# 512-column joint products for high and low activations in a three-part float32r matrix product kernel

## What is computed

```python
proj = n @ w_in
h = x + jnp.concatenate([gla_out, nsa_out], axis=-1) @ w_out
m = rms_norm(h, ffn_norm_g)
return h + (jax.nn.silu(m @ w_gate) * (m @ w_up)) @ w_down
```

## Time and profile before

| | |
|---|---|
| median of 3 runs | 2099.07 us (2090.81 to 2099.28) |
| the profiled execution | 2097.16 us, span 2095.2 us |
| granted TensorE clock, mean | 0.984 of full speed |
| PE busy | 2040.4 us, 97% |
| PE weight loads | 1988.4 us, 95% |
| DVE busy | 1561.3 us, 75% |
| ACT busy | 895.0 us, 43% |
| memory traffic | 434.46 MB, mean 207 GB/s |

### The profile page before, as it was taken

How to read it: one execution, slowest core, us unless ns; L and a number is a source line. 1 busy time by engine, 2 the same in 40 slices (tenths; PEclk the granted TensorE clock), 3 DMA queues, 4 the chain that set the end, 5 groups by cost and what they waited for, 6 DMA issues and landing times.

```text
span 2095.2 us, 41764 instructions
## 1 busy us (share of the span) xinstructions
PE 2040.4 (97%) x16266; PEld 1988.4 (95%) x16266; DVE 1561.3 (75%) x2056; ACT 895.0 (43%) x1178; POOL 171.9 (8%) x264
## 2 busy tenths in 40 slices
PE   7999999999999999999999998999999997999997
PEld 6999998899999999999999998998889996999996
DVE  6985576657777867787878888678887777677755
ACT  6553446554343334333333454235454444344442
POOL 0000000021000000000011111010000120000010
PEclk9999999999999999999999999999999998999998
DMA  6444453255666776666878864565556772558552
GB/s 229 161 162 136 167 184 119 101 178 205 230 228 224 261 277 222 228 224 236 272 259 295 299 224 172 172 247 197 199 171 224 262 274 105 192 204 277 195 187 98
DMA packets 119578, 434.46 MB, mean 207 GB/s; under 512 B 13216, under 2 KB 13600, under 8 KB 119216
## 3 DMA queue, kind: packets, MB, share of 16 engines
q1 hardware_dynamic: 90672, 328.11, 45.8%
q0 software_dynamic: 28800, 104.87, 14.2%
HBM read 430.83 MB, written 2.10 MB: 207 GB/s over the span
## 4 chain that ended last, share of the span: by engine, by line
PE 90%; DVE 7%; ACT 1%; issue 1%; DMA 1%; POOL 0%; SPq 0%; POOLq 0%; DVEq 0%; ACTq 0%
PE ps L565 27%; PE ps L567 26%; PE ps L566 26%; DVE w_lo L1407 2%; PE ps L644 1%; PE ps L968 1%; PE ps L639 1%; PE ps L978 1%; PE ps L683 1%; ACT w_hi L1062 0%; DVE pr L1563 0%; PE ps L674 0%; PE ps L919 0%; PE ps L650 0%; DVE rstd L1472 0%
## 5 line engine op out<-in xcount | busy, mean ns | idle before, releaser
L1062 ACT ACTIVATE w_hi<-raw 128x1024 fp32r<-128x1024 f32 x610 | 632.3, 1055 | 638.0 <-PE ps L567 625.5
L565 PE MATMUL ps<-a_hi,w_hi 128*128 128x256 f32 x3024 | 865.2, 286 | 6.3 <-DVE a_lo L1490 4.3
L566 PE MATMUL ps<-a_lo,w_hi 128*128 128x256 f32 x3024 | 858.3, 284 | 0.0
L567 PE MATMUL ps<-a_hi,w_lo 128*128 128x256 f32 x3024 | 858.1, 284 | 0.0
L1407 DVE TENSOR_TENSOR w_lo<-raw,w_hi 128x1024 fp32r<-128x1024 f32 x610 | 734.8, 1246 | 109.7 <-ACT w_hi L1062 108.6
L565 PEld LDWEIGHTS ps<-a_hi,w_hi 128*128 128x128 f32 x3024 | 583.2, 193 | 12.3 <-issue 7.5
L566 PEld LDWEIGHTS ps<-a_lo,w_hi 128*128 128x128 f32 x3024 | 583.4, 193 | 1.0 <-issue 1.0
L567 PEld LDWEIGHTS ps<-a_hi,w_lo 128*128 128x128 f32 x3024 | 583.0, 193 | 0.0
L565 PE MATMUL ps<-b_hi,w_hi 128*128 128x256 f32 x1920 | 553.6, 288 | 5.2 <-DVE b_lo L1490 4.6
L566 PE MATMUL ps<-b_lo,w_hi 128*128 128x256 f32 x1920 | 546.5, 285 | 0.0
L567 PE MATMUL ps<-b_hi,w_lo 128*128 128x256 f32 x1920 | 546.5, 285 | 0.0
(11 more groups left out here) (308 smaller groups left out, 1291.2 us busy)
## 6 DMA issues: line engine op xcount, KB each, us to landing
raw<-w_main SPq DMA_DIRECT2D x610, 512.0 KB, 4.3
side<-w_side POOLq DMA_DIRECT2D x200, 512.0 KB, 4.5
x_tok<-x_in SPq DMA_DIRECT2D x4, 512.0 KB, 7.4
ctx_tok<-ctx_tok SPq DMA_DIRECT2D x1, 2048.0 KB, 11.4
y_out<-o_tok SPq DMA_DIRECT2D x4, 512.0 KB, 3.2
table<-counts_tab SPq DMA_DIRECT2D x1, 512.0 KB, 12.9
cons<-cons_in SPq DMA_DIRECT2D x1, 478.0 KB, 10.4
table<-masks_in SPq DMA_DIRECT2D x1, 448.0 KB, 10.3
```

Source lines behind the costliest of these rows:

```text
L565: pe.matmul(out_ap, wh, act_hi[:, kt, :], start=first and n == 0, stop=False)
L566: pe.matmul(out_ap, wh, act_lo[:, kt, :], start=False, stop=False)
L567: mm = pe.matmul(out_ap, wl, act_hi[:, kt, :], start=False, stop=last and n == len(blocks) - 1)
L1062: act.activation(w_hi[:, slot, :], raw[:, slot, :], ACT.Copy).then_inc(hi_ready, 1)
```

## The change

Three things change. In the ten stages of `JOINT` the high and the low part of an activation tile lie side by side (`a_act`, `b_act`), and the two products with `w_hi` become one of 512 columns that fills a whole PSUM bank; the third stays at 256 columns. So columns 256 to 511 of the bank hold the part from the low activations. ACT copies that part to the destination tile (`low_half`) once the step's products are done, and DVE adds the two parts (`sum_read`, `scaled_sum_read`, `kv_read`, `up_read`) where it copied or scaled one. The SiLU moves from the gate's step to the up tile's. At the start the first weights are rounded between the tiles of the input, and the norm of x moves behind, its product into the middle of step 1.

```diff
+JOINT = ("gout", "nkv", "up0", "up1", "up2", "up2b", "ev_kv", "ev_q", "ev_q2", "od_u")
+def low_outs(stage, k):
+    return sum(COUNT[n] for n in JOINT[:JOINT.index(stage)]) + k + 1
...
+        a_act = at("a_act", A, [P, 16, 2, T], F32R)
+        a_hi, a_lo = a_act[:, :, 0, :], a_act[:, :, 1, :]
...
+            def joint_products(bank, c, par, act, first, last, split=None):
+                slot = 2 * par + c
+                for b in range(8):
+                    wh, wl = w_hi[:, slot, b * P:(b + 1) * P], w_lo[:, slot, b * P:(b + 1) * P]
+                    kt = 8 * c + b
+                    if split is not None:
+                        pe.wait_ge(S(split[0]), split[1] + kt + 1)
+                    pe.matmul(ps[:, bank, :], wh, act[:, kt, :, :], start=first and b == 0, stop=False)
+                    mm = pe.matmul(ps[:, bank, 0:T], wl, act[:, kt, 0, :], start=False, stop=last and b == 7)
+                return mm
...
+                    if s == 1 and c == 1:
+                        pe.wait_ge(S("x_diag"), 1)
+                        pe.wait_ge(S("x_fd"), 3)
+                        pe.matmul(ps[:, 2, 0:T], ones, x_diag[:, :, :], start=True, stop=True).then_inc(S("x_rb"), 1)
                     pe.wait_ge(lo_ready, i * 4 + (2 * s + c + 1))
...
+            def low_half(stage, i, k, dst):
+                s = FIRST[stage] + k
+                act.wait_ge(halves_used, i * 4 + (2 * s + 2))
+                act.wait_ge(dve_read, i * 2 + (dve_reads(stage) + k))
+                for n, tile in enumerate(dst(k)):
+                    ins = act.activation(tile, ps[:, 2 * n + s % 2, T:2 * T], ACT.Copy)
+                ins.then_inc(S("low_out"), 1)
...
                     if extra is not None:
                         extra(i, k)
+                    if low is not None:
+                        low_half(stage, i, k, low)
...
+            x_squares(0)
+            act.wait_ge(S("cols_in"), 16)
+            x_rounded(0)
+            x_squares(1)
+            x_rounded(1)
+            hi(0, 0, (0,))
+            x_rounded(2)
+            hi(0, 0, (1,))
             x_rounded(3)
...
-                if g >= 3:
-                    x_rest(g - 3)
...
+                if g == 6:
+                    lo(0, 0, (0,))
+                if g >= 2:
+                    x_rest(g - 2)
+            lo(0, 0, (1,))
+            for g in range(6, 8):
                 x_rest(g)
...
-                        dve.tensor_tensor(up_x[:, k % 2:k % 2 + 1, :], psum_tile(bank), rstd_row, ALU.mult)\
-                           .then_inc(dve_read, 1)
+                        y = up_x[:, k % 2:k % 2 + 1, :]
+                        dve.wait_ge(S("low_out"), low_outs(name, k))
+                        then(dve.tensor_tensor(y, psum_tile(bank), y, ALU.add))
+                        dve.tensor_tensor(y, y, rstd_row, ALU.mult).then_inc(dve_read, 1)
```

More of the change, by code:

```diff
@@ L873, in _ @@
             run("last", (a_hi, a_lo), split=[("x_lo", 0)], chain=chain)
-            for stage in ("conv", "gout", "nkv", "nq"):
-                run(stage, (a_hi, a_lo), chain=chain)
+            run("conv", (a_hi, a_lo), chain=chain)
+            for stage in ("gout", "nkv"):
+                run(stage, a_act, chain=chain)
+            run("nq", (a_hi, a_lo), chain=chain)
             pe.wait_ge(S("g_out"), 4)
@@ L993, in _ @@
             pe.wait_ge(S("ctx_lo"), 8)
-            run("ev_kv", (b_hi, b_lo), second=(a_hi, a_lo), split=[("norm_lo", normed("ev", -1)), None], chain=chain)
-            run("ev_q", (b_hi, b_lo), chain=chain)
-            run("ev_q2", (b_hi, b_lo), chain=chain)
+            run("ev_kv", b_act, second=a_act, split=[("norm_lo", normed("ev", -1)), None], chain=chain)
+            run("ev_q", b_act, chain=chain)
+            run("ev_q2", b_act, chain=chain)
             run_z("ev_z", 0, (b_hi, b_lo), chain=chain)
@@ L1269, in _ @@
             chain = l1_chain()
-            for stage in ("last", "conv", "gout", "nkv", "nq", "outg", "outn"):
+            for stage in ("last", "conv"):
+                ahead(stage, chain=chain)
+            ahead("gout", chain=chain, low=lambda k: [pr[:, GOUT + k, :]])
+            ahead("nkv", chain=chain, low=lambda k: [pr[:, NKC + k, :]])
+            for stage in ("nq", "outg", "outn"):
                 ahead(stage, chain=chain)
```

126 lines of the change are left out of this document (70 added, 56 removed).

## The result

The changed kernel takes 2068.94 us (median of 4 runs, 2067.14 to 2076.81), the kernel before 2098.19 us beside it: a ratio of 0.988, with a 95% interval from 0.986 to 0.990. It is faster by 1.2%. The profiled execution took 2069.66 us, with a span of 2067.7 us and a mean granted clock of 0.986. The forecast was 2066.

What follows compares the result with a forecast made beforehand. PE was taken to bound the kernel, busy for 97% of the span. 2097.16 - 30.0 (joint products) - 2.5 (start) + 1 (given away in up2 and up2b) = 2065.7, said as 2066 us; range 2036 to 2092.

Steps and rivals of the forecast that it cites:

- The joint product: Joint stages: 2496 triples of 360 ns become pairs of 228 + 120 = 348 ns, 30.0 us saved.
- The splitting of the 13 ns: Loss per 256-column float32r start: 3 ns a record, 6 with the load behind, 4 with the product itself.
- The rivals of the price: Other prices of the 512-column product: 216 ns, nothing lost (chance 0.15), or 240, loss grows with columns (0.20).
- nothing rode along: Rival: the second 256 columns cost next to nothing, a pair takes 240 ns, about 1915 us; chance 0.05.
- The cover of copy and addition: Joint steps: ACT's copy and DVE's added work are hidden behind PE, with 1.3 us remaining in a pair of up0 steps.
- the walk: Pair of up0 steps followed through ACT and DVE: last `lo` operations at 9.8 and 11.0 us, PE wants the first at 11.14.
- The slower rival: ACT's copy in series: PE waits 0.5 us in each of 148 joint steps, 74 us, total 2139; chance 0.10.
- The 1 us given away in up2 and up2b: Over 24 steps there: DVE at 5.27 of 5.57 us a step and transfers needing 310 GB/s cost 1 us.
- No row in which PE waits for `w_lo` inside the joint stages: Sign expected in the changed trace, all joint stages: PE never waits for the rounded low weights.
- The start: Kernel start: first weight product near 18.6 us, 3.9 earlier, part of it lost; gain 2.5 us, between 0 and 4.
- the first rival: Joint stages: the joint product loses nothing, 216 ns for 512 columns, total 2037 us; chance 0.15.
- the second: Joint stages: the loss grows with the columns, 240 ns, only the start's gain remains, 2095 us; chance 0.20.

Runs made afterwards that it cites:

- The grouped order: Changed kernel with, in each half of a step, the eight 512-column products first, then the eight of 256: 2071.73 us, ratio 0.990 to the kernel before.
- half the traffic: Changed kernel with each modulation tile's transfer cut to half its columns: 2066.90 us, ratio 0.986 to the kernel before.
- the start alone: Kernel before with only the new start, every triple as before: 2092.18 us against 2095.61, ratio 0.9985.

## Why the prediction came out right

- **The joint product: the mechanism right, the size close.** 228 + 120 = 348 ns for a pair was forecast, 349.9 is the mean of the changed kernel: (360 - 349.9) x 2496 = 25 us instead of 30.0. The splitting of the 13 ns said that 9 of them come once for a product and 4 once or twice. The grouped order measured the same thing directly, 230 and 119; 17 ns are 9 + 2 x 4, the upper end of the 226 to 230. That 6 of the 9 go with the weight load is not shown: no run took the load away, and it was read from the durations of matmuls (273, 277, 283 ns), whose ends are modelled in these profiles. The measured price rests on starts alone. What was not foreseen is that a pair has two lengths, 347 and 353, which run through whole stages; the 832 pairs of up0, up2 and ev_q2 stood near 353.
- **The rivals of the price fell.** 216 and 240 are both outside what any stage shows (230 to 237), and nothing rode along.
- **The cover of copy and addition: right.** DVE's timeline follows the walk, no kernel with or without the copy differs in up0, and a copy 0.44 us longer stayed hidden. The slower rival needed 0.5 us a step; it is excluded.
- **The 1 us given away in up2 and up2b: mis-sized.** The prediction had both parts of the reason (DVE at 5.27 of 5.57 us a step, and 292 GB/s where shorter steps ask for 310) but put it at 1. It measured 1.70 us in up2b and 1.96 at down2's start, 3.7 in all. The runs with half the traffic and without the copy show late side tiles and DVE's fuller steps behind the first, the side tiles behind the second. So the three stages gained nothing: 219.4 us before, 219.9 after. In the other joint kernels with the copy and the full traffic the waits in up2 and up2b are 0.5 to 1.8, where there are any, and the one in down2 1.3 to 2.5. The long ones in down2 may cost twice: in the twelve profiles with the sums in rows, the clock fell behind down2's row of 16 one-column products in the four where PE had waited 1.7 to 2.1 us just before it, the changed kernel's among them (1.5 us more), and in none of the others, with 1.6 us of waiting or less.
- **A place that was not looked at:** nq, which is no joint stage, got 1.0 us longer. PE waits 1.14 us for `k_cmp`, which DVE makes behind the last reads of nkv; without copy and addition that wait is gone, but which of the two delays it was not followed further. "No row in which PE waits for `w_lo` inside the joint stages" failed in up2b; a second row, 1.12 us at the start of od_u, stood in the kernel before too (1.08).
- **The start: right.** 2.9 us by the stage, 3.4 by the medians of the start alone (0.4 to 6.1 by its interval), against 2.5. PE begins the weights at 17.92, where 18.6 was said, 4.6 us earlier than before. 28 of its starts, up to 23.9 us, are at the lower clock, where it was some 11 before: 17 x 93 ns = 1.6 us are lost again; the prediction named this loss.
- **The clock: not in the sum.** The lower granted clock moved 6.1 us between the two profiled executions, in favour of the changed kernel: down0, up1, down1 and ev_kv had less of it, down2 more. With it the terms are 25.3 (pairs) - 1.7 (up2b) - 1.8 (the rest of the joint stages, 1.3 of it in ev_kv, not followed) + 2.9 (start) - 1.0 (nq) - 1.9 (down2) - 0.4 (conv) + 6.1 (clock) = 27.5 us, the difference of the spans. Without it the change is worth some 21 us, ten less than the forecast sum; that the forecast of 2066 met the time within 3 us owes much to this. The other executions say the same. Of those of the kernel before beside the experiments, fourteen had a mean clock of 0.986 and took 2092.6 us on average; the two of the changed kernel at 0.986 took 2070.5, 22 us less, and at 0.984 and 0.985 the difference is 22.5 and 20.1. The rest of the medians' 29 us goes with the clock: on average 0.984 in these 42 executions of the kernel before and 0.986 in nine of the changed one. Whether that is luck or of the change's making is not known; other kernels with the joint products had 0.982 or 0.988. Over all profiled executions the lower clock held for 54 to 83 us, 13 us of time between the ends.
- **The range says little.** 2036 to 2092 takes in the first rival (2037) and nearly all that lies towards the second (2095). What bears the forecast out is the price of a pair and the stages, not that the time lies inside.

## What to carry to other kernels

Where a stationary operand is used twice, one product over both moving parts saves what is lost once for each product, here some 13 ns of each 256-column start at the full clock and nothing at the lower one; the columns themselves cost what they did, so count 10 ns a merged product and not half of it. Before crediting the gain to a stage, look at what else flows in it: where the transfers' share was already 0.87, a step shorter by 3% gave all of it back: the tiles of another queue came late, the engine that uses them had more work of its own, and TensorE waited for that engine, in part one stage further on. And in a kernel whose clock dips at a dozen places, read each stage at equal clock; a difference of totals under some 10 us can be the dips alone.

## What the runs showed of the hardware that was not expected

- Pairs of a 512- and a 256-column float32r product go at either 347 or 353 ns, mostly for a whole stage (346, 347, 347 or 349, 350, 361 in turn); with eight of a kind in a row the means are 230.1 and 119.1 ns, 349 in every stage.
- At 40 of 48 rows of 32 one-column products (about 0.11 us apart) the granted clock fell from 2.4 to 1.2 GHz for 3.4 or 6.8 us; behind rows of 16 it never fell in five stages, and in down2 in four of twelve profiles, those in which PE had waited 1.7 to 2.1 us just before. With two of them within each block of wide products no fall stood at the four places (1.00 in all three windows), with four in each block of the second run of a half one did, in up2 (3.4 us).
- ACT's copies of 32 columns, eight in a row, take 0.83 us together: they overlap, and eight small ones cost little more than twice one of 256 (0.39).
